# Router logits taken from x times (1 + scale), squares summed on the vector engine, and the first expert tile picked by one-hot matmuls

## The reference

```python
ctx = ctx + m_ctx[2] * o_ctx                       # residual, per token set
h   = modulate(rms_norm(x, norm2_g), shift, scale)  # y*g*(1+scale)+shift
# hier_moe(h):
g_prob   = softmax(h @ w_grp + b_grp);  g_p, g_i = top_k(g_prob, 1)
e_logits = (h @ w_rt + b_rt)[group g_i];  e_p, e_i = top_k(softmax(e_logits), 2)
gates    = one_hot(4*g_i + e_i) * g_p * e_p / sum(e_p)
y = sum_e gates[e] * ((silu(h @ w_gate[e]) * (h @ w_up[e])) @ w_down[e])
x = x + m[5] * y
```

## Time and profile before

| | us |
|---|---|
| median of 3 runs | 1243.19 (1240.71 to 1245.28) |
| the profiled execution's own time | 1242.03 |
| its span, first to last instruction | 1240.2 |
| PE busy | 1118.2 (90%) |
| DVE busy | 381.9 (31%) |
| ACT busy | 235.2 (19%) |
| POOL busy | 94.3 (8%) |

### The profile page before, as it was taken

One profiled execution on the slowest core, in us unless ns is written; L12 is line 12 of the kernel. 1 busy time (PEld: TensorE's weight loads), 2 busy tenths in 40 slices (PEclk: granted clock), 3 DMA queues, 4 the chain that ended last, 5 costly groups with the idle time before them and its releaser, 6 DMA issues.

```text
span 1240.2 us, 13275 instructions
## 1 busy us (share of the span) xinstructions
PE 1118.2 (90%) x5022; PEld 530.7 (43%) x5022; DVE 381.9 (31%) x974; ACT 235.2 (19%) x510; POOL 94.3 (8%) x164
## 2 busy tenths in 40 slices
PE   4898899999999769988999989999898699789997
PEld 1444455455546433333333344445654333233334
DVE  2332204245363521111111154553744311111114
ACT  4221110333322300000000132233533100000001
POOL 0000020101000001100110110000000111001110
PEclk9898999999999879999999999999999799899999
DMA  8854483423675925999969852211039599999972
GB/s 358 343 203 179 182 313 139 176 109 148 236 315 215 420 111 234 426 428 425 398 275 379 353 231 77 90 66 65 1 119 422 190 428 424 428 413 426 416 281 96
DMA packets 32982, 326.87 MB, mean 264 GB/s; under 512 B 6234, under 2 KB 7386, under 8 KB 15008
## 3 DMA queue, kind: packets, MB, share of 16 engines
q1 hardware_dynamic: 21744, 295.94, 57.8%
q0 software_dynamic: 11184, 30.19, 6.6%
HBM read 314.02 MB, written 22.28 MB: 271 GB/s over the span
## 4 chain that ended last, share of the span: by engine, by line
PE 77%; DMA 15%; DVE 4%; ACT 2%; issue 1%; POOL 0%; DVEq 0%; ACTq 0%; POOLq 0%
PE bank L1714 19%; PE bank L1627 13%; PE bank L1730 10%; DMA arena<-in_moe 9%; PE bank L1619 9%; PE bank L1914 7%; DMA ring<-in_proj 4%; PE bank L1587 2%; PE bank L1604 2%; PE bank L1675 2%; PE bank L1836 1%; PE bank L1743 1%; PE bank L1771 1%; DMA h_rows<-hT 1%; PE bank L1881 1%
## 5 line engine op out<-in xcount | busy, mean ns | idle before, releaser
L1714 PE MATMUL bank<-arena,cT 128*64 128x512 f32 x880 | 242.4, 605 | 6.4 <-DMA arena<-in_moe 6.3
L1627 PE MATMUL bank<-ring,hT 128*128 128x512 f32 x384 | 169.7, 597 | 3.0 <-ACT hT L770 3.0
L1714 PE MATMUL bank<-ring,cT 128*64 128x512 f32 x464 | 150.2, 609 | 8.6 <-DMA ring<-in_moe 5.3
L1714 PEld LDWEIGHTS bank<-arena,cT 128*64 128x64 f32 x880 | 78.3, 140 | 128.1 <-issue 127.3
L1730 PE MATMUL bank<-arena,hT 128*64 128x512 f32 x512 | 113.4, 595 | 12.3 <-ACT hT L830 9.6
L1619 PE MATMUL bank<-hT,ring 128*128 128x384 f32 x320 | 111.1, 508 | 10.8 <-DMA ring<-in_proj 8.3
L1627 PEld LDWEIGHTS bank<-ring,hT 128*128 128x128 f32 x384 | 72.1, 192 | 88.7 <-issue 86.3
L1375 DVE TENSOR_TENSOR hT<-bank,hT 128x512 f32<-128x512 f32 x21 | 14.5, 691 | 298.8 <-PE bank L1714 298.8
L1619 PEld LDWEIGHTS bank<-hT,ring 128*128 128x128 f32 x320 | 62.7, 198 | 56.5 <-issue 9.4
L1914 PE MATMUL bank<-cT,ring 128*128 128x384 f32 x256 | 85.0, 489 | 0.0
L1714 PEld LDWEIGHTS bank<-ring,cT 128*64 128x64 f32 x464 | 48.4, 140 | 82.7 <-issue 82.7
(11 more groups left out here) (281 smaller groups left out, 1105.8 us busy)
## 6 DMA issues: line engine op xcount, KB each, us to landing
arena<-in_moe SPq DMA_DIRECT2D x66, 2048.0 KB, 20.7
ring<-in_proj SPq DMA_DIRECT2D x41, 2048.0 KB, 10.7
ring<-in_moe SPq DMA_DIRECT2D x30, 2048.0 KB, 20.3
y_rows<-cT POOLq DMA_DIRECT2D x12, 512.0 KB, 8.0
arena<-y_rows POOLq DMA_DIRECT2D x12, 512.0 KB, 6.4
h_rows<-hT POOLq DMA_DIRECT2D x6, 512.0 KB, 6.9
arena<-in_hyconst SPq DMA_DIRECT2D x1, 2432.0 KB, 14.8
xT<-in_x SPq DMA_DIRECT2D x1, 1536.0 KB, 11.1
```

The lines of the kernel that those rows point to most:

```text
L1627: ins = mm(ps[:, :], src[:, k, P * i : P * i + P], w[:, k, :], start=k == 0, stop=k == KD - 1)
L1714: ins = mm(psum[kind][rows, :], mo["hS"][:, k, rows], w[side].rearrange("p (k n) -> p k n", k=KD)[:, k, :], start=k == 0, stop=k == KD - 1)
```

## The change

The change touches what stands between the last output product of a mixer and the first expert tile, in both layers:

- ACT squares each chunk into a buffer of its own and also writes `xT` times gain times (1 + scale) into `hT`. DVE adds six of the squares as they come (`add_square`), and PE multiplies only the sum and the last square by ones. The same sum is used in the norms in front of the mixers (`norm1`).
- The router's matmuls read this `hT`, which has neither norm factor nor shift. The factor per token comes from six one-column matmuls and is applied by DVE when it reads the logits; the part of the logits that comes from the shift is worked out apart (`shift_logits`, `shift_sum`).
- The full `hT` is finished later: POOL multiplies each chunk by `rs`, ACT adds the shift. Then the transposes to rows follow, in two halves of four chunks.
- The first tile is no longer gathered: PE multiplies the rows in SBUF by a one-hot matrix `pick`. Gathers begin with the second tile. The table has room for 20 tiles where it had 48.
- The two late modulation blocks are split around `rt`, and `put` is transposed behind pair 0.

```diff
-TILES = NPAIR * (OVER + 1)
+TILES = NPAIR + 2 * T // CAP
+def last_half(layer, half):
+    products = out_half(layer, half)
+    return [("shift_logits", layer), *products[:4], ("shift_sum", layer), *products[4:]]
@@ plan_banks
                 banks.take("ht", layer, i, half)
...
-                banks.take("adt", *step[1:])
+                banks.take("adt", *step[1:], bank=DOWN_BANK + step[2] % 2)
@@ POOL, set_up
+                full(pool, "rk", layer)
+                pool.wait_ge(rs_ready, 2 * layer + 2)
+                for k in range(KD):
+                    nc.gpsimd.tensor_tensor(hT[:, k, :], hT[:, k, :], rs[:, :], ALU.mult).then_inc(scaled, 1)
@@ POOL, experts
-                gather(idx[:, 0:1])
-                pool.wait_ge(sems["rows_full"], 2)
                 gather(idx[:, 1:2])
@@ ACT
+            def norm2(layer):
...
+                for k in range(KD):
+                    residual(act, count, k)
+                    if k >= 3:
+                        act.wait_ge(squares_added, ADDED * layer + k - 2)
+                    nc.scalar.activation(squares[k % 2][:, :] if k else square_sum, xT[:, k, :], ACT.Square).then_inc(squares_ready, 1)
+                    for s, seg in enumerate(SEGS):
+                        nc.scalar.activation(hT[:, k, seg], xT[:, k, seg], ACT.Copy, scale=gs[:, layer, 1, k, s : s + 1]).then_inc(gained, 1)
...
+                link(nc.scalar.activation(ln_tok, bank(*name)[:, T : T + NT], ACT.Ln, bias=eps, scale=1.0 / D))
+                nc.scalar.activation(rs_tok, ln_tok, ACT.Exp, scale=-0.5).then_inc(token_rs, 1)
+                full(act, "rk", layer)
+                nc.scalar.activation(mo["rk"], bank("rk", layer)[:, 0:T], ACT.Copy).then_inc(free_of("rk", layer), 1)
+                nc.scalar.activation(rs[:, :], bank(*name)[:, 0:T], ACT.Ln, bias=eps, scale=1.0 / D).then_inc(free_of(*name), 1)
...
+                nc.scalar.activation(rs[:, :], rs[:, :], ACT.Exp, scale=-0.5).then_inc(rs_ready, 1)
+                if layer == 0:
+                    modulation(*LATE_MODS[0][1:])
+                for k in range(KD):
+                    act.wait_ge(scaled, count * KD + k + 1)
+                    for s, seg in enumerate(SEGS):
+                        nc.scalar.activation(hT[:, k, seg], hT[:, k, seg], ACT.Identity, bias=mod[:, layer, 24 + k, s : s + 1]).then_inc(h_by_act, 1)
+                if layer == 0:
+                    modulation(*LATE_MODS[1][1:])
@@ ACT, experts
                 act.wait_ge(table_ready, layer + 1)
+                act.wait_ge(sems["rows_stored"], 16 * NT)
@@ DVE
+            def add_square(count, k, total):
+                dve.wait_ge(squares_ready, KD * count + k + 1)
...
             def add_out(layer, half, j):
                 if half == layer:
+                    if j >= 2:
+                        add_square(2 * layer + 1, j - 1, square_sum)
@@ DVE, route
-                V.tensor_tensor(lg, bank("rt", layer)[...], b_rt..., ALU.add).then_inc(free_of("rt", layer), 1)
+                for i in range(NT):
+                    ins = V.scalar_tensor_tensor(lg[:, i, :], bank("rt", layer)[:, FOLD * i : FOLD * i + 20], rs_tok[:, i : i + 1],
+                                                 shift_logit[:, min(i, 1), 0:20], ALU.mult, ALU.add)
...
+                link(V.scalar_tensor_tensor(mo["key"], at_tile, float(P), at_slot, ALU.mult, ALU.add))
+                for i in range(NT):
+                    ins = V.tensor_scalar(mo["pick"][:, i, :], ids, mo["key"][:, 0, i : i + 1], None, ALU.is_equal)
+                link(ins)
+                for i in range(NT):
+                    V.scalar_tensor_tensor(mo["pick"][:, i, :], ids, mo["key"][:, 1, i : i + 1], mo["pick"][:, i, :],
+                                           ALU.is_equal, ALU.add).then_inc(picked, 1)
@@ DVE, experts
                 route(layer)
+                for half in range(2):
+                    rows_out(half, 1)
+                addresses(layer)
@@ PE
+            def norm2(layer):
...
+                for k in range(KD - 1):
+                    raw_logits(k)
...
+                mm(ps[:, 0:T], ones, square_sum, start=True, stop=False)
...
+                mm(ps[:, 0:T], ones, last[:, :], start=False, stop=True)
+                for i in range(NT):
+                    mm(ps[:, T + i : T + i + 1], square_sum[:, token_tile(i)], ones[:, 0:1], start=True, stop=False)
+                    ins = mm(ps[:, T + i : T + i + 1], last[:, token_tile(i)], ones[:, 0:1], start=False, stop=True)
...
+                raw_logits(KD - 1).then_inc(full_of("rk", layer), 1)
@@ PE, experts
+                            if i == 0:
+                                h_ready(2 * layer + 1, 4 * half + k)
...
-                pe.wait_ge(table_ready, layer + 1)
+                pe.wait_ge(picked, NT * (layer + 1))
+                for k in range(KD):
+                    for i in range(NT):
+                        ins = mm(psum[ROWS_BANK + k // 4][...], h_rows[:, k // 4, i, P * (k % 4) : P * (k % 4) + P],
+                                 mo["pick"][:, i, :], start=i == 0, stop=i == NT - 1)
...
-                        rows_in(g + 1)
+                        rows_in(g)
```

More of the change, by code:

```diff
@@ L831, in experts @@
                                          ACT.Copy).then_inc(sems["hidT_ready"], 1)
+                full(act, "put", layer)
+                nc.scalar.activation(mo["scat"], bank("put", layer)[:, 0:T], ACT.Copy).then_inc(free_of("put", layer), 1)
                 end = first_tile(act, NPAIR)
-                act.wait_ge(sems["gathered"], end * 16 + 16)
+                act.wait_ge(sems["gathered"], end * 16)
                 act.wait_ge(weighed, layer + 1)
@@ L1983, in _ @@
                     out_part(*step[1:])
-            norm(1, 1)
+                elif kind == "shift_sum":
+                    shift_sum(u)
+            norm2(1)
             experts(1)
```

216 lines of the change are left out of this document (140 added, 76 removed).

## The result

| | before | changed |
|---|---|---|
| median of the runs | 1242.91 us (5 runs, 1238.37 to 1245.28) | 1234.98 us (5 runs, 1234.71 to 1238.11) |
| profiled execution | 1242.03, span 1240.2 | 1238.11, span 1236.3 |
| ratio of the runs | | 0.9942, 95% interval 0.9923 to 0.9962 |

Faster by 0.6%, inside the range, but with a gain of about half of the 15.1 forecast. The changed kernel was timed once more later, beside other experiments: 1236.41 against 1243.27 for before, ratio 0.9942 again (0.9922 to 0.9962).

What follows compares the result with a forecast made beforehand. PE carries 77% of the chain, so time is won in serial work before each layer's first gate: 5.0 + 9.9 + 0.5 - 0.3 = 15.1 off 1242.03 gives 1226.9, forecast as a median of 1228, range 1218 to 1239.

Steps and rivals of the forecast that it cites:

- Logits, route's start: DVE's route starts 6.2 (layer 1) and 7.4 us (layer 0) after the mixer's last output product; layer 1 had 14.45.
- POOL's products: Eight products finishing `hT`: 0.91 us each, bounds 0.46 and 1.37, the eighth ending at +13.7.
- Rival A: POOL is the bound: at 1.37 per product the last comes 3.7 later per layer; gain 7.7, 1235; chance 0.15.
- rival C: Slower: POOL products take far longer beside DVE's route; at 2.3 each, 1250; chance 0.05.
- The rule that I cited against the change: Two-input DVE and SBUF-reading GpSimd instructions block each other fully; route could lose about three microseconds, within its slack of 3.7.
- The counting in layer 1: Counting matmuls behind the last transposes start at +16.0, set by PE's order; DVE goes on at +17.3, before +21.6.
- The pick: PE's 24 one-hot matmuls, 48 records, from +22.9 and +24.3: 7.1 us, bounds 5.4 and 11.5.
- The step that failed: Between `slots` and first gate: only DVE's two short instructions and a hop, 0.4 us; gate at +31.6 and +33.0.
- The first gate pair no longer pays for the low clock: First gate and up block falls from 14.68 to 13.73 us, 0.9 gained per layer.
- Rival B: PE stays at the low clock through pick, slots and first gate: 7.0 per layer, gain about 1, 1242; chance 0.10.
- Norms in front of the mixers: Squares summed by DVE: a loss of 0.3 us between the layers and a gain of 0.5 at the start.
- DMA: Layer 0: the row stores' wait, moved before ACT's first Silu, is hidden; tile 2's gather (8.20) fits beside first gate and up.

Runs made afterwards that it cites:

- Registers early: Changed kernel with PE reading the first pair's tile bounds before waiting for the pick, and no wait for `slots` to be read: 1229.72 us, ratio to before 0.9888.
- slots inside the pick: Changed kernel with early register reads, and the `slots` matmuls moved between the two halves of the pick: 1227.63 us, ratio to before 0.9871.
- three fillers: Changed kernel plus three unread matmuls behind `slots`, before the wait for the table: 1234.75 us, again 1233.61 beside the changed kernel's 1236.41.
- count early: Changed kernel with the three counting matmuls placed before the second half of the transposes instead of behind them: 1234.60 us, ratio to before 0.9945.
- eight fillers: Changed kernel plus eight unread matmuls of ones in PE's wait before the pick: 1238.19 us, ratio to before 0.9956.

## Why the prediction was wrong in its sum, and what of it was right

The range held the result, but neither the forecast nor a rival describes it: POOL and the logits came as forecast, and what was lost lay between `slots` and the end of the first gate and up block.

- **Logits, route's start: right.** DVE's first logit instruction came at +6.5 in layer 1 (945.36) and +7.6 in layer 0, forecast +6.2 and +7.4.
- **POOL's products: right.** 0.96 each, forecast 0.91, between 0.46 and 1.37. Rival A did not come, nor rival C: beside DVE a product took no longer than alone. The rule that I cited against the change (the Trainium skill, SBUF — State Buffer, Who interferes with whom) holds for DVE's side alone: the route before the counting grew from 5.93 to 9.2 (layer 1) and 9.9 (layer 0), near the three microseconds reckoned from it. The trace agrees there in part: a two-input step of 0.21 took 0.95, and one-input steps (L1345, 0.87) waited too. As forecast, its slack of 3.7 covered that in layer 1. In layer 0 it was just used up: the counting there is released by DVE (L1360), at +17.6 against a forecast of 17.1. That is one of the signs of being wrong that the prediction named, "DVE ready for the counting after PE is"; it cost about half a microsecond.
- **A reading that was wrong:** "The trace has no DVE work beside a POOL instruction that reads". It has: POOL's copies (L707, four in 2.60) run beside DVE's L1199 in the mixer of layer 0, and all 80 instances of L1199 took 0.33 to 0.35, beside a copy or not. L1199 reads one operand in SBUF and one in PSUM, so this row tells nothing of two SBUF operands.
- **The counting in layer 1: 1.4 late.** The last nine transposes took 2.18 where I had taken 0.11 each. PE had waited in short pieces for ACT's chunks, and the clock was low.
- **The pick: right in length,** 7.16 and 7.36 (forecast 7.1), with the clock rising in its fourth microsecond. It began at +24.0 in both layers, 0.3 sooner than forecast in layer 0 and 1.1 later in layer 1 (from the counting). Its worth was mostly in layer 0. The row that its low part was taken from was read 0.7 short: PE was at work there from 975.73 on (L1700), not from 976.4.
- **The step that failed** is "two short DVE instructions with a hop, 0.4. First gate at +31.6 (layer 1) and +33.0 (layer 0)". It took 2.02 in layer 1 and 3.07 in layer 0. Before the change PE had three `put` and eight row transposes (L1700, L1675) between `slots` and the first gate. I took these off PE's path and counted only what DVE does then, 0.3 in layer 1, where the forecast has 0.4. But PE's stream also reads the tile bounds into registers and enters the loop, and I put this at nothing. Before, it lay under the transposes, which end at 978.31, and the gate began at 978.32:

```profile
976.40 1.91 PE L1675 MATMUL bank<-con,cT 128*128 128x128 f32 x8
```

With nothing queued behind `slots` it lies bare, 1.7 in layer 1 and 2.2 in layer 0; the rest in layer 0 is DVE's reads of the modulation (0.5), which the forecast's 0.4 left out too. "Registers early" takes away most of it, and with the clock below it is most of the 6 to 8 us that this edit and "slots inside the pick" bring.
- **The same step, second half:** "The first gate pair no longer pays for the low clock". It did, more than before: 16.63 and 15.57 against 14.68 and 14.61. I had let the clock rise in the pick, which it did, and stay up, but it fell in the gap or just behind it in 12 of 14 such blocks, and in no block where the gap was filled or gone. Together gap and clock took 4.3 + 4.7 of the forecast's gain in the profiled execution (gap 3.07 + 2.02 less 0.4 each; blocks less 13.73 each). Rival B had the low clock in the first gate, but through pick and `slots` too, and those ran at the high level when they ended.
- **Norms in front of the mixers:** forecast -0.3 and +0.5, measured -1.0, and +0.3 against the kernel before or +0.8 against the old norm in the changed kernel. PE waits 3.27 for DVE's last add and then does its first matmul at a low clock (1.62 for two records, where sixteen took 5.33).
- **DMA: right.** The wait for the row stores was hidden, and the second tile's gather too. The tenth weight block was issued 4.9 sooner:

```profile
475.09 0.81 SPq L615 DMA_DIRECT2D arena<-in_moe  x2
```

- **What is won in front of the loop reaches the end: right.** From the second tile's gate to the first block behind the long weight waits it is 127.1 before (473.08 to 600.16), 126.8 in the changed kernel's second trace (468.31 to 595.13) and 127.1 with three fillers (463.83 to 590.89). In the first trace it is 129.4, from one slower block there (10.05, where before it was 8.80 and elsewhere 7.10). The other trace of the same kernel doesn't show that, so I count it as scatter.

In sum, by the profiled execution: S gained 5.2 and 0.8, where the forecast's S has 10.6 and 5.7 (14.9 in all when `shift_sum` and `put` are taken off). Of the 10.4 missing, gap and clock are 9.0, and the later counting in layer 1 most of the rest. Medians say 7 to 8 in all, the two traces 3.9: before's profiled execution was 1.2 below its median and the changed kernel's 2.2 above. These 3.4 us between traces and medians are not explained, and they are as large as half the gain.

## What to carry to other kernels

When work is taken off an engine, ask what it had been covering: here eleven transposes had hidden the engine's register reads, and had given its clock time to rise before the long block began. Move such reads in front of an earlier wait, or put a piece of real work behind the result that the next step waits for. Fillers pay only where they fit inside a wait: three in the gap cost nothing and the clock stayed up in all four cases, eight in front of the pick overran it and gave it all back. A shift to another engine that is covered in time may still slow a third one, here 3 us of DVE beside POOL, which its slack covered in layer 1 and all but covered in layer 0.

## What the runs showed of the hardware

- A DVE instruction with SBUF operands waits for a running POOL product, even with one input and 48 columns (L1345 0.87 for one input, L1346 0.95, the latter 0.21 alone); the wait is at most about one POOL instruction (0.88 beside products of 0.96, 0.35 beside pieces of 0.42). MAX8 and FIND_INDEX8 (0.17 each) were not slowed. POOL wasn't slowed at all (7.70 beside DVE, 7.68 alone).
- POOL's two-input product costs 0.96 for 384 columns and 0.42 (9.97 over 24) for 128: by these two, about 0.15 per instruction and 2.1 ns per column.
- Two loop bounds read from SBUF into PE's registers with no matmul queued leave PE idle for about 1.7: in layer 0 the gate follows DVE's last read by 2.24 with the reads there and by 0.54 with the reads made earlier.
- Behind the bare gap of 2.0 to 3.1 us, with the clock at its high level before it, the next 64 matmul records took 15.3 to 16.9 in 12 of 14 cases and 13.95 in two ("count early" layer 0, "eight fillers" layer 1). With three fillers in the gap they took 13.95 in four of four, with no gap 13.88 in seven of seven. Behind the 1.37 in layer 0 of "registers early" they took 15.65. What decides between the two outcomes of the bare gap is not shown.
